# Moving one weight tile 16 bytes along its partition rows in a two-block transformer kernel

## The chip, the cores and the metric

The kernel runs on one core of one Trainium2 chip. The metric is the device time of one execution in microseconds (us). Single instructions are given in nanoseconds (ns). The profile comes from one execution that the hardware profiler recorded.

## The reference

Two transformer blocks are applied one after the other to one sequence of 512 tokens of width 1024, in float32. The first block projects the normalised input, runs a latent attention and a grouped attention with rotary angles, merges them with sigmoid gates, and then applies a squared-ReLU feed-forward of width 4096 and a gated embedding. The second block is a gated delta rule layer with a gated feed-forward of width 2816, followed by a forgetting-attention layer with another such feed-forward. Cut to the form in which the weights matter:

```python
z = rmsnorm(x, g_mix) @ w_in                 # ... attention, gates
x = x + merged @ w_o
u = relu(rmsnorm(x, g_mlp) @ w_up);  x = x + (u * u) @ w_down
...
gu = rmsnorm(x, g) @ w_ffn_in
x = x + rmsnorm((silu(gu[:, :2816]) * gu[:, 2816:]) @ w_ffn_out, g2)
```

Nearly all of the work is a product of a 512-row activation with a weight matrix.

## The kernel before

**Weights.** All weight matrices are packed on the host into 165 chunks, each at most 128 partitions by 2048 float32 values (8 KB of each partition). The chunks stream through a ring of two slots. For chunk n, SyncE loads it into `weights_raw` (line 199, up to two chunks ahead), ScalarE rounds it to the matmul's input type into `weights_high` (L223), and VectorE writes the remainder, raw minus high, into `weights_low` (L250). Chunk n uses slot n % 2 of each of the three tiles. SyncE waits for `low_ready` of chunk n - 2 before it loads chunk n, ScalarE waits until the last product that reads chunk n - 2 is done, VectorE waits for ScalarE, and TensorE waits for VectorE (`low_ready`). Three chunks are kept in tiles of their own, `early_high` and `early_low`.

**Products.** Each activation is also split into a high and a low part (`split`, `hidden`, `merged` and others). A product is then three matmuls that add up in one PSUM bank: high by high (L441), weight-high by activation-low (L442), and weight-low by activation-high (L443). At the start of some stages the same three stand at L452, L456 and L453. The first operand of `matmul` is the stationary one, loaded by a weight load (PEld), and the second is the moving one. In the names of the profile the moving operand stands first: `psum<-split,weights_low` has `weights_low` stationary. In the last feed-forward the two sides are exchanged, so `weights_low` is the moving operand there (L442, `psum<-weights_low,hidden`), and also in a few projections. Nearly every matmul of this kind has 128 stationary columns and 512 moving columns. One matrix has only 16 columns (the decay logits, `128*16`, where the piece of contraction tile k begins 64 * k bytes into the chunk) and one has 80 (`128*80`, the forget logits, whose piece begins at column 176 of 256, which is 704 bytes in).

**Order in memory.** Along each partition row the tiles stand in the order in which they are declared: `weights_raw`, `weights_high`, `weights_low` (16,384 bytes each), then `const` (259 values: an identity, a column of ones and others), `gains` (110 values), `conv` (96 values), a tile `arena_offset` that nothing reads or writes (40 values), `x_stream`, and the rest. Each tile begins at a multiple of 32 bytes, the same rounding that the class `Stage` reckons with:

```python
self.at += (4 * math.prod(shape[1:]) + 31) // 32 / 32
```

Rounded so, `const`, `gains`, `conv` and `arena_offset` take 1,056 + 448 + 384 + 160 = 2,048 bytes.

**Order of work.** Stages follow one another, each with its own program for every engine; the order within an engine is written out by hand. Nothing in it depends on addresses.

Of the kernel before, what the change touches and what calls it, by code (L numbers as in the profile page):

```python
# [4 lines left out]
P = 128  # L5
# [23 lines left out]
FOX_HEADS, FOX_HD = 16, 64  # L29
D_FF2 = 2816  # L30
CHUNK = 2048
SOLVE = 32
EXPONENT_LIMIT = 40.0
NEG = -1.0e30
# [19 lines left out]
for _name, _n in [("identity", P), ("heads_of_pair", 2), ("ones", 1), ("causal_bias", P),  # L54
                  ("earlier", P), ("before", P), ("not_after", P), ("eye", SOLVE * SOLVE)]:
    CONST_AT[_name] = (_col, _n)
# [5 lines left out]
def shape_constants():  # L62
# [3 lines left out]
    def put(name, value):  # L66
        at, n = CONST_AT[name]
        c[:, at:at + n] = value
# [11 lines left out]
    put("not_after", np.where(row <= col, EXPONENT_LIMIT, NEG))  # L80
    put("eye", np.eye(SOLVE).reshape(1, SOLVE * SOLVE))
    return c
# [20 lines left out]
class Chunk:  # L103


    def __init__(self, first, i=0, per_turn=0):
        assert per_turn % 2 == 0
        self.slot = first % 2
        self.number = first + i * per_turn if per_turn else first
        self.uses = first // 2 + 1 + i * (per_turn // 2) if per_turn else first // 2 + 1  # L110
        self.first, self.i, self.per_turn = first, i, per_turn
# [39 lines left out]
class Weights:  # L151


    def __init__(self, nc, enter, plan, packed):
        from concourse import mybir
        self.nc, self.plan, self.packed = nc, plan, packed
        f32, f32r = mybir.dt.float32, mybir.dt.float32r
        self.f32, self.sub = f32, mybir.AluOpType.subtract
        self.raw = enter(nc.sbuf_tensor("weights_raw", [P, 2, CHUNK], f32))
        self.high = enter(nc.sbuf_tensor("weights_high", [P, 2, CHUNK], f32r))  # L160
        self.low = enter(nc.sbuf_tensor("weights_low", [P, 2, CHUNK], f32r))
        self.loaded = [enter(nc.semaphore(f"weights_loaded_{s}")) for s in range(2)]
        self.high_ready = enter(nc.semaphore("weights_high_ready"))
        self.low_ready = enter(nc.semaphore("weights_low_ready"))

        self.products = enter(nc.semaphore("products_done"))
        self.apart = {}
        self.start = {}
        n = 0
        for name, segments in plan:  # L170
            self.start[name] = n
            n += sum(turns * len(items) for turns, items in segments)
        self.total = n
        self.width, self.tiles_before, tiles = [], [0], 0
        for _, segments in plan:
            for turns, items in segments:
                for i in range(turns):
                    for kt, cols, count in items:
                        self.width.append(kt * cols)
                        tiles += count  # L180
                        self.tiles_before.append(tiles)
# [177 lines left out]
def pack_weights(plan):  # L359

    chunks, shapes = [], []
    for name, segments in plan:
        shapes.append((name, [(turns, [(kt, cols, count) for kt, cols, _, count in items]) for turns, items in segments]))
        for turns, items in segments:
            for i in range(turns):
                for kt, cols, part, _ in items:
                    chunk = np.zeros((P, CHUNK), np.float32)
                    chunk[:, 0:kt * cols] = part(i).reshape(P, kt * cols)
# [23 lines left out]
def build_program(nc, w, plan, constants, tables, out):  # L392
# [4 lines left out]
    f32, f32r, bf16 = mybir.dt.float32, mybir.dt.float32r, mybir.dt.bfloat16  # L397
# [3 lines left out]
    enter = ctx.enter_context  # L401


    def place(name, at, shape, dtype=mybir.dt.float32):

        under = int(at * 256)
        if under == 0:
            with nc.sbuf_tensor(name, shape, dtype) as tensor:
                return tensor
        with nc.sbuf_tensor(name + "_under", [P, under], mybir.dt.float32), nc.sbuf_tensor(name, shape, dtype) as tensor:  # L410
            return tensor
# [5 lines left out]
    with ctx:  # L417
# [1 line left out]
        const = enter(nc.sbuf_tensor("const", [P, N_SMALL_CONST], f32))  # L419
        gains = enter(nc.sbuf_tensor("gains", [P, N_GAINS], f32))  # L420
        conv = enter(nc.sbuf_tensor("conv", [P, N_CONV], f32))
        enter(nc.sbuf_tensor("arena_offset", [P, 40], f32))
        x = enter(nc.sbuf_tensor("x_stream", [P, DT, T], f32))
        square_sum = enter(nc.sbuf_tensor("square_sum", [P, T], f32))
        psum = enter(nc.psum_tensor("psum", [P, 8, T], f32))
# [1679 lines left out]
        def gdn_project(ahead_of, split, qkv, z2, lower, columns, scratch, kept, spare, inverses):  # L2105
# [26 lines left out]
            with stage("gdn_in", 133) as s:  # L2132
# [35 lines left out]

                X, step_product, M = [scratch[:, 2 * n:2 * n + 2, :].rearrange("p a (b c) -> p (a b) c", c=SOLVE) for n in range(3)]

# [3 lines left out]
                with nc.Block() as block:  # L2174
                    @block.sync
                    def _(sp_):
# [20 lines left out]
                        for n in range(TT):  # L2197
                            sp_.wait_ge(lower_ready, 2 * n + 2)
                            for r in range(4):
                                at = slice(r * SOLVE, (r + 1) * SOLVE)  # L2200
                                sp_.dma_start(solver_rows[r, n].rearrange("h s t -> s h t"), lower[at, n, :, at]).then_inc(blocks_out, 16)
                            if n == 1:
                                weights.load(sp_, start + 13)
                        at = CONST_AT["eye"][0]
                        sp_.dma_start(X.rearrange("p a b -> p (a b)"), constants[:, at:at + SOLVE * SOLVE]).then_inc(eye_in, 16)
                        sp_.wait_ge(blocks_out, 16 * 4 * TT)
# [6 lines left out]
                        weights.load(sp_, weights.end("gdn_in"))  # L2213
                        sp_.wait_ge(taken, SOLVE - 1)
                        sp_.dma_start(inverse_out.rearrange("r n h i c -> (r n h) (i c)"), X.rearrange("p a b -> p (a b)")).then_inc(written, 16)
# [1110 lines left out]

        early = [place(name, at, [P, CHUNK], f32r) for name, at in (("early_high", 0), ("early_low", 8))]
        for name in ("ffn0", "fox_in", "ffn1"):
# [111 lines left out]
```

## Time and profile before

| | |
|---|---|
| time of the runs | 2163.68, 2167.99, 2168.05 us, median 2167.99 us |
| the profiled execution | 2162.32 us |
| its span, first to last instruction | 2160.5 us |
| mean granted TensorE clock | 0.987 of 2.4 GHz |
| DMA | 190.68 MB, mean share of the 16 engines 0.26 |

The span is what the trace shows, and 1.8 us of the execution lie around it. An engine's busy time is the union of its instructions' durations. Matmuls are pipelined: one is listed with 389 ns from its start to its end, while the next starts some 227 ns after it. For TensorE the distance between starts is therefore the number to read.

### The profile page before, as it was taken

How to read it: one execution, taken by the hardware profiler on the slowest of the kernel's cores; microseconds unless marked ns; L12 is line 12 of the kernel's file. 1: busy time of each engine (PE TensorE's matmuls, PEld its weight loads, DVE VectorE, ACT ScalarE, POOL GpSimd, SP SyncE). 2: the span in 40 equal slices, each digit the busy share in tenths (PEclk: the TensorE clock that was granted, in tenths of full speed). 3: DMA queues.
4: the chain of work that ended last, by engine and by line, in shares of the span. 5: the costliest groups of instructions: out<-in, count | busy, mean ns of one | idle time of the engine just before them, and what ended most of it. 6: DMA issues, size and time to landing. Idle time of an engine off the chain costs nothing. (4 is left out here: it accounts for less than half of the span.)

```text
span 2160.5 us, 26090 instructions
## 1 busy us (share of the span) xinstructions
PE 2095.5 (97%) x10710; PEld 1697.5 (79%) x10710; DVE 1146.3 (53%) x1706; ACT 816.6 (38%) x1169; POOL 38.4 (2%) x34
## 2 busy tenths in 40 slices
PE   8999999999999999999999999999999899999998
PEld 6876678888888887787878888887786577888886
DVE  5674765542542579888846444324634736444423
ACT  4324753331232465542534222213325734322212
POOL 0120000000000000000100000000000000000000
PEclk9999999999999999999999999999999999999999
DMA  4220012223223222233122222222240031222221
GB/s 177 86 83 35 2 59 99 94 95 109 85 96 103 91 81 100 108 117 97 40 98 74 95 95 94 95 96 95 98 173 23 1 118 59 98 98 98 98 98 68
DMA packets 43111, 190.68 MB, mean 88 GB/s; under 512 B 15520, under 2 KB 16224, under 8 KB 22384
## 3 DMA queue, kind: packets, MB, share of 16 engines
q1 hardware_dynamic: 40656, 184.78, 25.0%
q10 hardware_dynamic: 2336, 4.23, 0.6%
q8 instruction: 85, 1.39, 0.3%
q14 instruction: 34, 0.28, 0.0%
HBM read 185.25 MB, written 3.74 MB: 87 GB/s over the span
## 5 line engine op out<-in xcount | busy, mean ns | idle before, releaser
L250 DVE TENSOR_TENSOR weights_low<-weights_raw,weights_high 128x2048 fp32r<-128x2048 f32 (+1 forms) x161 | 365.8, 2272 | 565.4 <-ACT weights_high L223 565.3
L441 PE MATMUL psum<-split,weights_high 128*128 128x512 f32 x1448 | 568.3, 392 | 8.3 <-PEq L146 4.2
L442 PE MATMUL psum<-split,weights_high 128*128 128x512 f32 x1448 | 564.6, 390 | 0.0
L443 PE MATMUL psum<-split,weights_low 128*128 128x512 f32 x1448 | 564.6, 390 | 0.0
L223 ACT CAST weights_high<-weights_raw 128x2048 fp32r<-128x2048 f32 (+1 forms) x161 | 304.0, 1888 | 545.3 <-PE psum L443 504.7
L441 PEld LDWEIGHTS psum<-split,weights_high 128*128 128x128 f32 x1448 | 272.2, 188 | 70.3 <-issue 8.4
L443 PEld LDWEIGHTS psum<-split,weights_low 128*128 128x128 f32 x1448 | 272.0, 188 | 57.4
L442 PEld LDWEIGHTS psum<-split,weights_high 128*128 128x128 f32 x1448 | 272.0, 188 | 56.0
L443 PE MATMUL psum<-hidden_high,weights_low 128*128 128x512 f32 x256 | 99.6, 389 | 0.0
L441 PE MATMUL psum<-hidden_high,weights_high 128*128 128x512 f32 x256 | 99.6, 389 | 0.0
L442 PE MATMUL psum<-hidden_low,weights_high 128*128 128x512 f32 x256 | 99.6, 389 | 0.0
L2042 ACT ACTIVATE ring<-ring 128x512 f32<-128x512 f32 x44 | 27.8, 632 | 117.4 <-DVE ring L2072 117.4
L441 PE MATMUL psum<-hidden,weights_high 128*128 128x512 f32 x176 | 68.5, 389 | 0.0
L442 PE MATMUL psum<-hidden,weights_high 128*128 128x512 f32 x176 | 68.5, 389 | 0.0
L442 PE MATMUL psum<-weights_low,hidden 128*128 128x512 f32 x176 | 68.5, 389 | 0.0
L441 PE MATMUL psum<-weights_high,hidden 128*128 128x512 f32 x176 | 68.5, 389 | 0.0
L443 PE MATMUL psum<-hidden,weights_low 128*128 128x512 f32 x176 | 68.5, 389 | 0.0
L443 PE MATMUL psum<-weights_high,hidden 128*128 128x512 f32 x176 | 68.5, 389 | 0.0
L452 PE MATMUL psum<-split,weights_high 128*128 128x512 f32 x112 | 48.0, 428 | 17.3 <-DVE weights_low L250 10.2
L2530 DVE SCALAR_TENSOR_TENSOR gdn_spare<-psum,conv,gdn_spare 128x511 f32<-128x511 f32 (+2 forms) x72 | 53.8, 747 | 11.0 <-ACT gdn_spare L2363 9.3
L938 DVE TENSOR_REDUCE attn_small<-psum 128x1 f32<-128x512 f32 x64 | 42.5, 688 | 30.6 <-PE psum L876 30.6
L442 PEld LDWEIGHTS psum<-hidden_low,weights_high 128*128 128x128 f32 x256 | 48.0, 188 | 10.1
(485 smaller groups left out, 3081.4 us busy)
## 6 DMA issues: line engine op xcount, KB each, us to landing
weights_raw<-in_weights SPq DMA_DIRECT2D x161, 1024.0 KB, 4.9
minus_c<-minus_c_rows ACTq DMA_DIRECT2D x16, 256.0 KB, 7.3
x_stream<-in_x SPq DMA_DIRECT2D x4, 512.0 KB, 7.1
gdn_in_grown<-gdn_rows SPq DMA_DIRECT2D x4, 512.0 KB, 4.7
chain_grown<-gdn_rows SPq DMA_DIRECT2D x4, 512.0 KB, 3.7
out<-end_results SPq DMA_DIRECT2D x8, 256.0 KB, 2.1
table<-rope_tables SPq DMA_DIRECT2D x1, 1024.0 KB, 12.0
weights_raw<-in_weights SPq DMA_DIRECT2D x1, 768.0 KB, 4.2
```

What stands on the lines that cost most here:

```text
L223: self.nc.scalar.copy(self.high_of(chunk.first)[:, 0:width], self.raw[:, chunk.slot, 0:width]).then_inc(self.high_ready, 1)
L250: self.nc.vector.tensor_tensor(out=self.low_of(n)[:, 0:width], in0=self.raw[:, n % 2, 0:width], in1=self.high_of(n)[:, 0:width].bitcast(se ...
L441: nc.tensor.matmul(bank, wh, ah, start=first, stop=False)
L442: nc.tensor.matmul(bank, wh, al, start=False, stop=False)
L443: return nc.tensor.matmul(bank, wl, ah, start=False, stop=last)
L452: nc.tensor.matmul(psum[:, bank, :], wh[:, k, sl], xh, start=k == 0, stop=False)
L938: nc.vector.tensor_reduce(small[:, 0, u:u + 1], psum[:, u % 4, 0:n], AX.X, ALU.max, negate=True).then_inc(max_ready, 1)
L2042: nc.scalar.activation(self.tanh[:, f % 2, :], self.gate[:, f % 2, :], ACT.Tanh, scale=0.5).then_inc(self.tanh_ready, 1)
L2530: nc.vector.scalar_tensor_tensor(out=mixed[:, o % 2, back:T], in0=psum[:, bank_of(o), 0:T - back], scalar=conv[:, at:at + 1], in1=mixed[:, ...
```

## The change

`weights_low` becomes a tile that is 4 float32 values (16 bytes) longer, and its two slots begin 16 bytes behind its start. `arena_offset` shrinks from 40 to 32 values, so that `x_stream` and all that follows keep their addresses.

```diff
+LOW_OFFSET = 4
...
-        self.low = enter(nc.sbuf_tensor("weights_low", [P, 2, CHUNK], f32r))
+        low = enter(nc.sbuf_tensor("weights_low", [P, LOW_OFFSET + 2 * CHUNK], f32r))
+        self.low = low[:, LOW_OFFSET:].rearrange("p (s c) -> p s c", s=2)
...
-        enter(nc.sbuf_tensor("arena_offset", [P, 40], f32))
+        enter(nc.sbuf_tensor("arena_offset", [P, 32], f32))
```

The tile is now 16,400 bytes long, rounded up 16,416. So `const`, `gains` and `conv` begin 32 bytes further on than before, and 32 + 1,056 + 448 + 384 + 128 = 2,048 bytes bring `x_stream` to its old place.

## Rows read from the trace of the kernel before

**Rows 1.** The page, part 1: busy time, share of the span, instructions.

```profile
PE 2095.5 (97%) x10710; PEld 1697.5 (79%) x10710; DVE 1146.3 (53%) x1706; ACT 816.6 (38%) x1169; POOL 38.4 (2%) x34
```

**Rows 2.** The chain that ended last, from 1740 us to the end, by line.

```profile
by line: PE psum L443 30.0%; PE psum L441 29.9%; PE psum L442 29.9%; DVE end_results L1901 1.3%; PE psum L452 1.1%; PE psum L453 1.1%; PE psum L456 1.0%; PE psum L1832 0.8%; DVE end_results L1882 0.7%; DVE weights_low L250 0.5%; DVE last_en
```

**Rows 3.** Who reads or writes weights_low: ns min/median/max; first, last start.

```profile
L443 PEld LDWEIGHTS psum<-split,weights_low x1448: 147/188/330, 23.9 to 2031.0; 128*128 128x128 f32 x180, 128*80 128x80 f32 x1
...
L442 PE MATMUL psum<-weights_low,hidden x176: 389/389/390, 2031.7 to 2150.7; 128*128 128x512 f32 x176
L250 DVE TENSOR_TENSOR weights_low<-weights_raw,weights_high x161: 282/2291/2661, 7.9 to 2131.6; 128x2048 fp32r<-128x2048 f32 x158, 128x1536 fp32r<-128x1536 f32 x1, 128x1024 fp32r<-128x1024 f32 x1, 128x128 fp32r<-128x128 f32 x1
...
L442 PE MATMUL psum<-weights_low,split x128: 387/389/398, 955.0 to 1644.3; 128*128 128x512 f32 x128
```

**Rows 4.** Whole span: busy us (instructions) of those that touch weights_low; clock, DMA.

```profile
0.00:2160.50 2160.50, 996.69 (x2548) 480.22 (x2548) 365.84 (x161) 0.99 0.26 88
```

**Rows 5.** Timeline of PE, 1400.4 to 1402 us: weights stationary; start, duration.

```profile
1400.48 0.39 PE L441 MATMUL psum<-hidden,weights_high 128*128 128x512 f32 x1
1400.71 0.39 PE L442 MATMUL psum<-hidden,weights_high 128*128 128x512 f32 x1
1400.94 0.39 PE L443 MATMUL psum<-hidden,weights_low 128*128 128x512 f32 x1
...
1401.84 0.39 PE L441 MATMUL psum<-hidden,weights_high 128*128 128x512 f32 x1
```

**Rows 6.** Timeline of PE, 2050 to 2051.5 us: weights moving.

```profile
2050.07 0.39 PE L442 MATMUL psum<-weights_low,hidden 128*128 128x512 f32 x1
2050.30 0.39 PE L443 MATMUL psum<-weights_high,hidden 128*128 128x512 f32 x1
...
2051.43 0.39 PE L442 MATMUL psum<-weights_low,hidden 128*128 128x512 f32 x1
```

**Rows 7.** Timeline of PE, 1531.1 to 1534.5 us: 80 stationary columns.

```profile
1531.16 0.39 PE L441 MATMUL psum<-split,weights_high 128*80 128x512 f32 x1
...
1534.33 0.39 PE L443 MATMUL psum<-split,weights_low 128*80 128x512 f32 x1
```

**Rows 8.** Timeline of PE, 810.6 to 814.4 us: 16 stationary columns.

```profile
810.83 0.40 PE L441 MATMUL psum<-first_split,weights_high 128*16 128x512 f32 x1
...
814.31 0.27 PE L1661 MATMUL psum<-const,gdn_in_final_stat 128*128 128x128 f32 x1
```

**Rows 9.** Groups by line and form: VectorE with SBUF operands 12, 8, 4 bytes in.

```profile
L2530 DVE SCALAR_TENSOR_TENSOR gdn_spare<-psum,conv,gdn_spare 128x510 f32<-128x510 f32 x24 | 18.0, 748 | 0.8
L2530 DVE SCALAR_TENSOR_TENSOR gdn_spare<-psum,conv,gdn_spare 128x509 f32<-128x509 f32 x24 | 17.9, 748 | 0.8
L2530 DVE SCALAR_TENSOR_TENSOR gdn_spare<-psum,conv,gdn_spare 128x511 f32<-128x511 f32 x24 | 17.9, 746 | 9.3 <-ACT gdn_spare L2363 9.3
```

**Rows 10.** The instructions on gains: the same operation, 512 elements, aligned start.

```profile
L1793 DVE SCALAR_TENSOR_TENSOR ring<-psum,gains,factor x18: 739/744/747, 1132.3 to 1793.7; 128x512 f32<-128x512 f32 x18
```

**Rows 11.** Timelines of ACT and of DVE, 1386 to 1401 us.

```profile
1387.14 1.91 ACT L223 CAST weights_high<-weights_raw 128x2048 fp32r<-128x2048 f32 x1 [3.22 <-PE psum L443]
...
1398.02 1.91 ACT L223 CAST weights_high<-weights_raw 128x2048 fp32r<-128x2048 f32 x1 [7.46 <-PE psum L443]
...
1389.08 2.29 DVE L250 TENSOR_TENSOR weights_low<-weights_raw,weights_high 128x2048 fp32r<-128x2048 f32 x1 [4.44 <-ACT weights_high L223]
```

**Rows 12.** Who waited for whom, PE's: us in total, times, longest.

```profile
PE psum L452 <- DVE weights_low L250: 10.2, 1, 10.2
...
PE psum L441 <- DVE weights_low L250: 5.6, 7, 1.7
```

**Rows 13.** Whole span: busy us (instructions) of those that read const.

```profile
0.00:2160.50 2160.50, 114.17 (x888) 96.18 (x888) 1.30 (x6) 0.99 0.26 88
```

**Rows 14.** The instructions on const: columns of ones and of heads, whose starts differ.

```profile
L1135 PE MATMUL psum<-const,square_sum x48: 164/250/251, 22.8 to 1808.5; 128*128 128x1 f32 x48
...
L566 PE MATMUL psum<-const,row_squares x48: 165/251/252, 65.0 to 84.4; 128*128 128x2 f32 x48
```

**Rows 15.** Windows 62 to 157 and 1376 to 1496 us: busy of PE, PEld, DVE, ACT, POOL.

```profile
62.00:157.00 95.00, 93.69 (x501) 76.16 (x500) 66.03 (x89) 28.30 (x32) 20.26 (x16) 1.00 0.26 89
...
1376.00:1496.00 120.00, 119.84 (x529) 98.91 (x527) 34.07 (x22) 30.68 (x26) 0.00 (x0) 1.00 0.31 105
```

## The prediction

> **What bounds the kernel now.** I read the page first, then the chain, then everything that touches the moved tile. The page has TensorE busy for 97% of the span, VectorE for 53%, ScalarE for 38% [rows 1]. The chain from 1740 us on is 30.0 + 29.9 + 29.9 = 89.8% the three matmuls of a product, and 0.5% the subtraction that writes weights_low [rows 2]. So time is set by the distance between the starts of matmuls, and by the few places where TensorE waits.
>
> That distance is the number to watch. With weights stationary, six matmuls start between 1400.48 and 1401.84 us: 1.36 / 6 = 226.7 ns each [rows 5]. With weights moving, six take 2051.43 - 2050.07 = 1.36 us, again 226.7 ns [rows 6]. 512 columns at the granted 2.4 GHz (clock 1.00 in these stretches [rows 15]) are 213.3 ns, so each matmul has 13.4 ns on top of its columns. Weight loads take 188 ns [rows 3], which leaves 39 ns of each distance free.
>
> **The change part by part.** No instruction, semaphore, wait, DMA or byte of traffic is added or removed, and no queue changes its order. What changes is the start address of some operands. Four kinds of access touch moved tiles.
>
> 1. weights_low as stationary or moving operand: 2548 matmuls and as many weight loads [rows 4], of which 176 + 128 in two groups (and four more) have it moving [rows 3]. No row has a start 16 bytes off, so I bound the cost by rows with other starts. The piece with 80 stationary columns begins 704 bytes into its rows, an odd multiple of 64, while its moving partner begins in step with the tiles; its 14 matmuls take 1534.33 - 1531.16 = 3.17 us, 226.4 ns each [rows 7]: no difference. With 16 stationary columns, whose pieces start at multiples of 64 bytes, 15 matmuls take 814.31 - 810.83 = 3.48 us, 232.0 ns each [rows 8]: 5.3 ns more. The column count differs there too, and most of the 5.3 ns may be its, so I use them as an upper bound for what a start can cost. From below: at most all 13.4 ns could go, if they were two reads getting in each other's way. I take 0, because the distance is the same 226.7 ns for high and low, for stationary and moving, and for starts that are out of step by 64 bytes, which a conflict between two addresses would hardly give. The bounds are +5.3 and -13.4 ns, times 2548: +13.5 and -34.1 us.
>
> The Trainium skill speaks against zero here. Its page "TensorE: Matmul & The Clock Gate", section "Back-to-back issue gap", gives a gap of N/2.4 + 2.5 ns, 215.8 ns for 512 columns; the rows show 226.7, so this trace does not agree, and the 10.9 ns between them could be read as something that a better placement returns. By that page the sum would be an estimated -27.8 us in place of 0.
>
> 2. The subtraction that writes weights_low: 161 times, median 2291 ns [rows 3]. The nearest rows are VectorE operations whose SBUF operands start 4, 8 and 12 bytes in: 746, 748 and 748 ns for 511, 510 and 509 elements [rows 9], against 744 ns for 512 at an aligned start [rows 10]. So an odd start costs about 4 ns. 161 times 4 ns is 0.6 us of VectorE time. In a steady stretch it is covered: ScalarE begins its rounding at 1387.14, the subtraction ends at 1389.08 + 2.29 = 1391.37, and the chunk is read when the other slot's products end, at about 1398.02, where the next rounding begins [rows 11]. That is 6.6 us of cover, by TensorE working on the other slot. Without cover it counts at the 1 + 7 places where TensorE waits for it [rows 12]: 8 times 4 ns, 0.03 us. Behind the subtraction, SyncE's next load waits for low_ready; being 4 ns later it is lost in the same 6.6 us. Taken: 0.0 us, with 0 below.
>
> 3. const moves by 32 bytes, though the change's words say that all else stays. It is read by 888 matmuls [rows 13]. Two of its pieces already start in different places, the column of ones 520 bytes in and the two head columns 512 bytes in, and take 250 and 251 ns [rows 14]. Taken: 0; at 1 ns each either way it would be 0.9 us.
>
> 4. gains and conv are read as one value per partition, at starts that step by 4 bytes already; 18 such operations lie within 739 to 747 ns [rows 10]. Taken: 0.
>
> One more rule bears on item 2. The Trainium skill, "SBUF — State Buffer", section "Specifications (TRN2)", says that SBUF has 16-byte lines and that each crossing to a new line pays. A shift by 16 bytes is one whole line, so even the 4 ns of the odd starts would not arise; no row here has such a shift, so the trace neither confirms nor refutes it. By that page item 2 is an estimated 0 in place of 0.03 us.
>
> **The sum**: 2162.32 + 0 + 0.03 + 0 + 0 = 2162.4 us for an execution like the profiled one. That execution is 5.7 us below the median of the runs shown, 2167.99, and the four executions known lie between 2162.32 and 2168.05. I forecast for the median of new runs a value inside that band, nearer to the median than to the profiled one: 2167 us.
>
> **The rivals.**
>
> *A: matmuls that read the low half get slower.* If a stationary or moving read that is out of step with the tiles around it keeps TensorE at the distance seen in the 16-column piece, it costs the 13.5 us of item 1: 2162.3 + 13.5 = 2175.8 for an execution like the profiled one, 2181.5 from the median. For it speaks that the big tiles of before all stand in step modulo 2,048 bytes, so no row shows a pair out of step by less than 64 bytes. Against it speak the 80-column rows and that a weight load has 39 ns to spare. It decides from 1.7 ns per low matmul on, where 2548 of them make 4.3 us, 0.2%. Chance 0.07.
>
> *B: the subtraction gets slower.* It writes 2048 elements per lane while reading two tiles, and from now on the written place is out of step with the read ones. If each took twice 2291 ns, the 8 places where TensorE waits for it would grow by 2.29 us, 18.3 us together, and in stages where VectorE is busier, 66.03 of 95 us between 62 and 157 us [rows 15], more places would join. 2186 us or more from the median. Against it: starts at 4, 8 and 12 bytes cost 4 ns, not a doubling. It needs some 0.5 us per subtraction, 8 times 0.5 = 4.3 us, before it can be measured. Chance 0.03.
>
> *C: a conflict goes away.* If the 13.4 ns on top of the columns come from a weight load and a moving read meeting in memory, and 16 bytes part them, up to 34.1 us go, 2134 us from the median. The page on TensorE gives a nearly equal end, an estimated 2140 us. Against it speaks that the excess is still there with an 80-column and with a 16-column load, which read less than two thirds and an eighth of the bytes [rows 7, 8]; a conflict of reads should shrink with the bytes. Chance 0.04.
>
> *D: the change doesn't do what it says,* in that const, gains and conv move and not the low half alone. That is so by the sizes, but it is worth under 1 us either way and ends with my forecast.
>
> **How the numbers follow.** No measurable change holds 0.80. A measurement of this kernel can tell about 0.2%, 4.3 us, from no change; the executions of before alone differ by 5.7 us, so 0.06 is left for a difference of over 0.2% that has no cause in the change, half to each side. Faster: C 0.04 + 0.03 = 0.07. Slower: A 0.07 + B 0.03 + 0.03 = 0.13. The likeliest case's own range is 2161 to 2170 us. It holds 0.80 nearly alone; I widen it above to A, since the untried pairing is the largest unknown, and a little below for scatter: 2159 to 2182 us. C lies outside.
>
> **What the profile of the changed kernel would show.** If I am right: the distance of starts stays 226.7 ns where weights_low is stationary and where it is moving; weight loads of it stay at 188 ns; the subtraction stays within 4 ns of 2291 ns; the waits of TensorE for it stay at 10.2 and 5.6 us. Under A every third distance is longer, or all settle near 232 ns, and TensorE's busy time grows by 10 us or more with the same counts. Under B the subtraction's median grows visibly and the waits of TensorE for it with it. Under C the distances after or before the low matmuls fall towards 213 ns. What would make the prediction wrong is a dependence on the relative place of two tiles finer than 64 bytes, which no row of before can show.

## The result, and the profile after

The changed kernel is slower: 2191.64 us median of four runs (2182.59 to 2199.17) against 2166.6 us (2163.68 to 2168.05). The ratio is 1.0116, with a 95% interval of 1.0073 to 1.0158. Its own runs spread over 16.6 us, those of before over 4.4 us here and over 8.6 us (2159.76 to 2168.33) in all its undisturbed runs beside the experiments. The profiled execution took 2199.17 us, its span is 2197.4 us, 36.9 us more than before.

The first line is the page's busy times of the changed kernel. Its line numbers are two higher than before: L445, L443, L444 and L252 answer to L443, L441, L442 and L250.

```profile
PE 2134.7 (97%) x10710; PEld 1700.8 (77%) x10710; DVE 1147.3 (52%) x1706; ACT 816.7 (37%) x1169; POOL 38.4 (2%) x34
```

Against [rows 1] the counts are the same, VectorE and ScalarE are busy as long as before, and TensorE is busy 39.2 us longer. So the 36.9 us lie in TensorE's instructions and not in its waits.

The instructions on weights_low in the changed kernel (ns min/median/max, first and last start):

```profile
L445 PEld LDWEIGHTS psum<-split,weights_low x1448: 147/188/331, 24.6 to 2065.2; 128*128 128x128 f32 x180, 128*80 128x80 f32 x1
...
L444 PE MATMUL psum<-weights_low,hidden x176: 388/396/398, 2065.9 to 2187.7; 128*128 128x512 f32 x176
L252 DVE TENSOR_TENSOR weights_low<-weights_raw,weights_high x161: 284/2292/2530, 7.6 to 2168.1; 128x2048 fp32r<-128x2048 f32 x158, 128x1536 fp32r<-128x1536 f32 x1, 128x1024 fp32r<-128x1024 f32 x1, 128x128 fp32r<-128x128 f32 x1
```

A weight load still takes 188 ns and the subtraction 2292 ns in place of 2291 [rows 3]. The matmul with weights_low moving grew from 389 to 396 ns. TensorE's waits for the subtraction are as before, 10.0 and 5.1 us beside 10.2 and 5.6 [rows 12]:

```profile
PE psum L454 <- DVE weights_low L252: 10.0, 1, 10.0
...
PE psum L443 <- DVE weights_low L252: 5.1, 7, 1.1
```

What changed is the distance between starts. The timeline of PE in the changed kernel, in the stretch that answers to [rows 5]:

```profile
1450.06 0.39 PE L443 MATMUL psum<-hidden,weights_high 128*128 128x512 f32 x1
1450.29 0.40 PE L444 MATMUL psum<-hidden,weights_high 128*128 128x512 f32 x1
1450.53 0.39 PE L445 MATMUL psum<-hidden,weights_low 128*128 128x512 f32 x1
...
1452.15 0.40 PE L443 MATMUL psum<-hidden,weights_high 128*128 128x512 f32 x1
```

Nine starts take 2.09 us, 232.2 ns each, in place of 226.7 [rows 5]. And it is not every third distance that grew: between 1300 and 1500 us the mean distance behind L443, L444 and L445 is 230.8, 233.3 and 232.5 ns, so behind the matmuls that read only weights_high too. Over the whole trace the mean distance of 128 by 512 matmuls (those under 260 ns counted) is 231.5 ns against 226.9. For 3 times 2548 = 7644 matmuls, 4.6 ns each is an estimated 35 us, which is nearly all of the 36.9.

### The profile page after: what moved, and what is told of

Its sections match the earlier page's. It is cut to its first block and busy times, and to the rows that moved or that the text cites. A ratio compares the mean times of both kernels' runs of the same rounds, so it can differ in the third digit from the quotient of the medians.

```text
span 2197.4 us, 26090 instructions
## 1 busy us (share of the span) xinstructions
PE 2134.7 (97%) x10710; PEld 1700.8 (77%) x10710; DVE 1147.3 (52%) x1706; ACT 816.7 (37%) x1169; POOL 38.4 (2%) x34
## 5 line engine op out<-in xcount | busy, mean ns | idle before, releaser
L252 DVE TENSOR_TENSOR weights_low<-weights_raw,weights_high 128x2048 fp32r<-128x2048 f32 (+1 forms) x161 | 365.6, 2271 | 582.5 <-ACT weights_high L225 582.4
L443 PE MATMUL psum<-split,weights_high 128*128 128x512 f32 x1448 | 573.4, 396 | 8.6 <-PEq L147 4.5
L444 PE MATMUL psum<-split,weights_high 128*128 128x512 f32 x1448 | 572.2, 395 | 0.0
L445 PE MATMUL psum<-split,weights_low 128*128 128x512 f32 x1448 | 570.3, 394 | 0.0
L443 PEld LDWEIGHTS psum<-split,weights_high 128*128 128x128 f32 x1448 | 272.3, 188 | 77.6 <-issue 8.2
L445 PEld LDWEIGHTS psum<-split,weights_low 128*128 128x128 f32 x1448 | 272.3, 188 | 63.6
L444 PEld LDWEIGHTS psum<-split,weights_high 128*128 128x128 f32 x1448 | 271.9, 188 | 62.8
L444 PE MATMUL psum<-hidden_low,weights_high 128*128 128x512 f32 x256 | 101.1, 395 | 0.0
L445 PE MATMUL psum<-hidden_high,weights_low 128*128 128x512 f32 x256 | 100.8, 394 | 0.0
L443 PE MATMUL psum<-hidden_high,weights_high 128*128 128x512 f32 x256 | 100.6, 393 | 0.0
L445 PE MATMUL psum<-weights_high,hidden 128*128 128x512 f32 x176 | 69.6, 396 | 0.0
L444 PE MATMUL psum<-hidden,weights_high 128*128 128x512 f32 x176 | 69.5, 395 | 0.0
L444 PE MATMUL psum<-weights_low,hidden 128*128 128x512 f32 x176 | 69.3, 394 | 0.0
L445 PE MATMUL psum<-hidden,weights_low 128*128 128x512 f32 x176 | 69.3, 394 | 0.0
L443 PE MATMUL psum<-weights_high,hidden 128*128 128x512 f32 x176 | 69.2, 393 | 0.0
L443 PE MATMUL psum<-hidden,weights_high 128*128 128x512 f32 x176 | 69.2, 393 | 0.0
L454 PE MATMUL psum<-split,weights_high 128*128 128x512 f32 x112 | 47.5, 424 | 17.0 <-DVE weights_low L252 10.0
L443 PEld LDWEIGHTS psum<-hidden_high,weights_high 128*128 128x128 f32 x256 | 48.1, 188 | 11.5
```

The lines of the kernel that those rows point to most:

```text
L252: self.nc.vector.tensor_tensor(out=self.low_of(n)[:, 0:width], in0=self.raw[:, n % 2, 0:width], in1=self.high_of(n)[:, 0:width].bitcast(se ...
L443: nc.tensor.matmul(bank, wh, ah, start=first, stop=False)
L444: nc.tensor.matmul(bank, wh, al, start=False, stop=False)
L445: return nc.tensor.matmul(bank, wl, ah, start=False, stop=last)
L454: nc.tensor.matmul(psum[:, bank, :], wh[:, k, sl], xh, start=k == 0, stop=False)
```

## The experiments

Below, a tile is "at 16" when it begins 16 bytes further on than before, and two tiles are "in line" when both moved equally or, as the later runs show, by amounts that differ by 256 bytes. Two theories stood at first: (1) the relative place of the low half disturbs TensorE, (2) the shift of const, gains and conv does. Later ones were M (what counts is the place of a stationary operand against its moving one), S (that of the high half against the low half) and A (a tile's own address).

**const_only** moves const, gains and conv alone.

```diff
+        enter(nc.sbuf_tensor("before_const", [P, 8], f32))
         const = enter(nc.sbuf_tensor("const", [P, N_SMALL_CONST], f32))
...
-        enter(nc.sbuf_tensor("arena_offset", [P, 40], f32))
+        enter(nc.sbuf_tensor("arena_offset", [P, 32], f32))
```

> weights_low stays in its old place; an unused tile of 32 bytes ahead of const moves const, gains and conv by 32 bytes, and arena_offset gives the 32 bytes back. Theory 1 (the relative place of the low half is the cause): starts of matmuls 226.7 ns apart in every long stretch, time within 0.2% of before. Theory 2 (the shift of const, gains and conv is the cause): about 232.2 ns in the long stretches, 1 to 1.5% slower, as in the changed kernel.

Measured: 2163.93 us, ratio 0.9998 (0.9988 to 1.0009). Theory 2 is out. (The brackets here and below hold the 95% interval.)

**low_32, low_64, low_4** are the change with LOW_OFFSET = 8, 16 and 1, and arena_offset at 32, 24 and 32 values.

> As the change, but the low halves begin 32 bytes further on in place of 16. Theory 1a (what matters is the place modulo 32 bytes): 226.7 ns throughout, within 0.2% of before. Theory 1b (any step out of line with the neighbouring tiles by less than 64 bytes does it): about 232.2 ns in most stretches, about 1.2% slower. Theory 2 (const, gains, conv) gives 1.2% slower as well, so this run is to be read with the run that moves const alone.

> Only the low halves move, by 64 bytes. Theory M (weights and activations have to be in line modulo 64 bytes) and theory A (each tile's own address has to be a multiple of 64 bytes, as all were before): starts 226.7 ns apart, time within 0.2% of before. The 80-column piece of before, which begins 704 = 11 times 64 bytes in and ran at 226.4 ns, is why 64 and not more. A rival with a longer period (128 bytes up to 2,048): 1 to 2% slower.

> The low halves begin 4 bytes further on, a step inside a 16-byte line. M and A: out of line, so 1 to 2% slower; the extra line that each read then touches (one in 32 of a 512-byte load) could add 1 ns or less on top. If only whole lines of 16 bytes count (a step inside a line leaves the order of the lines nearly as it was), the time stays within 0.3% of before. The subtraction on VectorE: within 5 ns of 2291 ns by all theories.

Measured: low_32 2206.59 us, ratio 1.0198 (1.0179 to 1.0216). low_64 2192.56 us, 1.0132 (1.0116 to 1.0148). low_4 2205.58 us, 1.0193 (1.0178 to 1.0208). So 4 bytes cost as much as 32, and the expectation that 64 bytes are harmless failed for both theories that had it. The busy times of all engines in a 300 us window of low_64 (1200 to 1500 us) show it in a count: 1299 matmuls, where before had 1325 in an equal window of the same stage (1180 to 1480 us). Its columns are the window, its length, and busy us (instructions) of PE, PEld, DVE, ACT and POOL, then granted clock, DMA share and GB/s. First before, then low_64:

```profile
1180.00:1480.00 300.00, 300.00 (x1325) 248.43 (x1324) 115.65 (x105) 79.17 (x69) 0.00 (x0) 1.00 0.28 97
```

```profile
1200.00:1500.00 300.00, 300.00 (x1299) 243.72 (x1299) 110.87 (x101) 76.14 (x66) 0.00 (x0) 1.00 0.28 96
```

**high_16 and high_low_16** pad the high tile, the second the low tile too:

```diff
-        self.high = enter(nc.sbuf_tensor("weights_high", [P, 2, CHUNK], f32r))
+        high = enter(nc.sbuf_tensor("weights_high", [P, 4 + 2 * CHUNK], f32r))
+        self.high = high[:, 4:].rearrange("p (s c) -> p s c", s=2)
```

> Only the high halves begin 16 bytes further on; the low halves stay. Both theories S and M have this slower by 1 to 1.5%: S because the steps between high and low are again 16 bytes, M because two of three matmuls are out of line (M allows up to twice the cost of the change, some 2.4%). A third theory L (something peculiar to the low tile, as VectorE's write of it) expects no change.

> High and low halves both begin 16 bytes further on, so they are in line with each other and 16 bytes out of line with the activations. Theory S (the step from one stationary operand to the next, high to low, is what disturbs TensorE): 226.7 ns throughout, no change from before. Theory M (a stationary tile out of line with the moving tile is what disturbs it): all three matmuls are out of line, at least the 1.2% of the change, up to 3 times as much if the change paid for one third only.

Both expectations describe the kernels wrongly. The padded high tile is 32 bytes longer, so the low tile behind it moved as well: high_16 has the high halves at 16 and the low halves at 32 bytes, high_low_16 has them at 16 and 48. Measured: 2205.95 us, 1.0194 (1.017 to 1.0218), and 2205.3 us, 1.0192 (1.0175 to 1.0208). Neither tells S from M.

**arena_32 and weights_arena_32.** The first only raises arena_offset from 40 to 48 values, which moves all activations by 32 bytes. The second pads high and low by 8 values each and sets arena_offset to 32.

> All weight tiles, const, gains and conv stay; arena_offset grows by 32 bytes, so x_stream, square_sum and all activation tiles, and the three chunks kept apart, begin 32 bytes further on. Theories M and A both: about 233 ns between starts and 1.9% slower, as with the weights moved, except in the stretches that read the chunks kept apart, where M expects 226.7 ns (both sides moved together) and A expects 233 ns. A theory that the weight tiles alone matter: no change.

> High halves, low halves and all of the arena begin 32 bytes further on together; only the raw tile stays. Theory M (relative place of stationary and moving operand modulo 64 bytes): 226.7 ns, within 0.2% of before. Theory A (own address modulo 64 bytes): both operands are off, 233 ns or more, 1.9% slower or worse.

Measured: arena_32 2209.83 us, 1.0209 (1.0192 to 1.0226). With every weight tile untouched it is as slow as any, so it isn't something of the low tile or of how VectorE writes it. Where it reads the chunks kept apart, which moved together with the activations, it ran at 230.5 ns on the mean (139 distances), neither M's 226.7 nor A's 233. These matmuls alternate there, six by six, with six of a chunk that is out of line, so the stretch decides nothing. weights_arena_32 2208.74 us, 1.021 (1.0191 to 1.0228). It had the same fault as above: high at 32, low at 64, arena at 32. Among themselves these places are those of low_32, and the distances are alike too (228, 233 and 239 ns in turn in both), a first sign that only relative places count.

**both_16, both_64, all_32** lay high and low halves in one tile, so that they move together:

```diff
+        both = enter(nc.sbuf_tensor("weights_both", [P, 4 + 4 * CHUNK], f32r))
+        self.high = both[:, 4:4 + 2 * CHUNK].rearrange("p (s c) -> p s c", s=2)
+        self.low = both[:, 4 + 2 * CHUNK:].rearrange("p (s c) -> p s c", s=2)
```

(with 4, 16 and 8 values; arena_offset 32, 24 and 40).

> A correction first: in the two earlier kernels that padded the high tile, the pad also pushed the low tile on, so high_16 had the high halves at 16 and the low halves at 32 bytes, high_low_16 had them at 16 and 48, and weights_arena_32 had high at 32, low at 64 and the arena at 32. Here high and low halves lie in one tile that begins 16 bytes further on, so both are at 16 and the arena at 0. Theory M (weights against activations): about 233 ns, 1.9% slower. Theory S (high against low alone): 226.7 ns, no change.

> High and low halves both at 64 bytes, the arena at 0. low_64 was 1.3% slower. If that came from high and low being 64 bytes apart (S with a long period, M with a period of 64), this one is back at 226.7 ns and within 0.3% of before, as the 80-column piece (704 = 11 times 64 bytes in, high and low alike) ran in before. If M has a period above 64 bytes: 231 ns or more in the long stretches, 1.3% slower or worse.

> High and low halves, const, gains, conv and the arena all 32 bytes further on; only the raw tile stays. Theory M or S (relative places): 226.7 ns, within 0.2% of before. Theory A (own address modulo 64 bytes): 233 ns, 1.9% slower or worse. weights_arena_32 did not decide it, since its low halves were at 64.

Measured: all_32 2163.43 us, ratio 1.0 (0.9987 to 1.0012). With all operands 32 bytes on together nothing is lost, so theory A falls for steps of 32 bytes. The raw tile stayed, so its place against high and low doesn't matter either. both_64 2205.33 us, 1.0191 (1.0173 to 1.0209): high and low are in line with each other and 64 bytes out of line with the activations. S alone can't explain that; of the three theories M is left, with a period above 64 bytes. both_16 2197.07 us, 1.015 (1.0123 to 1.0176), between the two. Two windows of both_16, the feed-forward of the first block and that of the second, show that one kernel has both:

```profile
450.00:750.00 300.00, 300.00 (x1325) 248.43 (x1324) 115.24 (x109) 86.24 (x85) 0.00 (x0) 1.00 0.28 97
1200.00:1500.00 300.00, 300.00 (x1287) 242.93 (x1287) 110.06 (x99) 75.42 (x65) 0.00 (x0) 1.00 0.27 92
```

The first runs at 300 / 1325 = 226.4 ns, like before, and the second at 233.1 ns, with the same places.

**reads_alone** (one execution) has no engine but TensorE at work while the starts are read. It leaves out the whole computation and copies x to the output. Four prepared tiles are read in the order of the product, one line of the program for each set of offsets:

```python
for t in S: last = [(mm(banks[t], H(0, k, t % 2), A(0, k), start=k == 0, stop=False),
                     mm(banks[t], H(0, k, t % 2), B(0, k), start=False, stop=False),
                     mm(banks[t], L(16, k, t % 2), A(0, k), start=False, stop=k == 7)) for k in W][-1][-1]
```

> This kernel leaves out the whole computation; its output is a copy of x. TensorE alone reads prepared tiles in the order of the real product (high by high, high by low part, low by high), 72 matmuls for each of 35 sets of start offsets, then eight series with one matmul per step; no other engine works meanwhile. If the effect lies in TensorE's own two reads: about 226.7 ns with all offsets at 0, and 229 to 233 ns with the low halves at 4, 8, 16, 32, 48 or 64 bytes, in nearly the same size as in the full kernels. If it needs writes of VectorE, ScalarE or DMA beside it: 226.7 ns in every set. Time about 44 times 16.5 us and the first copy, some 750 us.

Measured: 679.49 us. The timelines of PE in reads_alone, the 12th and the last of each set of 72 starts: all at 0 (L74), low at 16 (L80), low at 64 (L86), low at 256 (L94), both at 64 (L104), and weights and activations all at 32 (L134).

```profile
27.05 0.39 PE L74 MATMUL psum<-moving_high,weights_low 128*128 128x512 f32 x1
...
40.65 0.39 PE L74 MATMUL psum<-moving_high,weights_low 128*128 128x512 f32 x1
...
77.82 0.39 PE L80 MATMUL psum<-moving_high,weights_low 128*128 128x512 f32 x1
...
91.76 0.40 PE L80 MATMUL psum<-moving_high,weights_low 128*128 128x512 f32 x1
...
129.01 0.40 PE L86 MATMUL psum<-moving_high,weights_low 128*128 128x512 f32 x1
...
142.88 0.40 PE L86 MATMUL psum<-moving_high,weights_low 128*128 128x512 f32 x1
...
196.98 0.39 PE L94 MATMUL psum<-moving_high,weights_low 128*128 128x512 f32 x1
...
210.58 0.39 PE L94 MATMUL psum<-moving_high,weights_low 128*128 128x512 f32 x1
...
280.81 0.39 PE L104 MATMUL psum<-moving_high,weights_low 128*128 128x512 f32 x1
...
294.81 0.40 PE L104 MATMUL psum<-moving_high,weights_low 128*128 128x512 f32 x1
...
534.86 0.39 PE L134 MATMUL psum<-moving_high,weights_low 128*128 128x512 f32 x1
...
548.46 0.39 PE L134 MATMUL psum<-moving_high,weights_low 128*128 128x512 f32 x1
```

Divided by 60 distances: 226.7, 232.3, 231.2, 226.7, 233.3 and 226.7 ns. No other engine works meanwhile; over 27 to 677 us of reads_alone, columns as in the windows above but without ACT:

```profile
27.00:677.00 650.00, 647.50 (x2774) 512.22 (x2773) 0.00 (x0) 0.00 (x0) 1.00 0.00 1
```

So the effect is TensorE's own, and it needs no write by VectorE, ScalarE or a DMA. It also has the size of the full kernel: 232.3 ns with the low halves at 16 bytes. And 256 bytes are in line again. Two more sets fit M well: with all activations at 64 the distance is 228.9 ns (L126), the same as with both weight halves at 192 (L108), and 192 is what 64 bytes to the other side are modulo 256.

Three series of reads_alone bear on the prediction's rows. With one matmul per step, all in line, 128 stationary columns ran at 226.7 ns, 64 columns at 230.0 and 16 columns at 231.7 ns. So with fewer stationary columns the distance was longer with nothing out of line.

**low_256** (LOW_OFFSET = 64, arena_offset 40, so the arena moves by 256 bytes too), **reads_pairs** (further series of the same kind, one execution; the computation is again left out) and **after_again** (the changed kernel once more) took up what was left.

> The low halves, const, gains, conv and the arena begin 256 bytes further on, raw and high stay. If only the places modulo 256 bytes count: 226.7 ns throughout, within 0.2% of before. If the tiles have to be in line over more than 256 bytes (512 to 2,048, as they all were before): 231 ns or more and 1 to 2% slower.

> Again the computation is left out and TensorE alone reads prepared tiles; the output is a copy of x. First 17 series of one matmul per step, the stationary operand 0 to 256 bytes from the moving one in steps of 16: 226.7 ns at 0, 16 and 256, 229 to 236 ns between. Then three series with 80 stationary columns: if the 80-column piece of before was in line by its own, 226.7 ns at 0 and at 192 bytes; if 192 bytes count as they do at 128 columns, 228.9 ns or more. Then the order of the stages' first chunk, with the low halves at 16 and 32 bytes. Last the product order with 8 different starts each for offsets 0, low 16, both 16: if a start decides whether a series settles, offset 0 settles at 226.7 ns in all 8, low 16 and both 16 in some and not in others; if not, all 8 of a kind end alike.

> The changed kernel once more, one look. If the start of a stretch decides whether it runs at 226.7 or at 232.2 ns, other stretches than in the first profile may run at 226.7 ns, and the time moves with their share, between 2180 and 2200 us: each 100 us of matmuls that settle save 2.4 us. If the place alone decided, the same stretches would run at 226.7 ns in both profiles.

Measured: low_256 2163.19 us, ratio 1.0004 (0.9991 to 1.0017). Its window from 1200 to 1500 us has 1326 matmuls, 226.2 ns:

```profile
1200.00:1500.00 300.00, 300.00 (x1326) 248.39 (x1325) 115.81 (x106) 82.26 (x75) 0.00 (x0) 1.00 0.30 100
```

In reads_pairs (725.76 us) one matmul per step ended at these mean distances, by how far the stationary operand stands from the moving one. Each column is one series of 48 matmuls per place:

| bytes | 0 | 16 to 64 | 80 | 96 | 112 | 128 | 144, 160 | 176 | 192 | 208, 224 | 240 | 256 |
|---|---|---|---|---|---|---|---|---|---|---|---|---|
| ns | 226.7 | 233.3 | 232.0 | 234.2 | 233.3 | 232.1 | 233.3 | 230.0 | 228.9 | 233.3 | 226.7 | 226.7 |

The expectation had 226.7 ns at 16 bytes, as the series of reads_alone with one matmul per step had run there; here it was 233.3 ns. So one series doesn't tell what a place always gives, and 240 bytes may be such a case as well. With 80 stationary columns it was 233.3 ns at 0 and 231.1 ns at 192 bytes. The order of a stage's first chunk ran at 226.7 ns in line, at 233.3 ns with the low half at 16 and at 231.8 ns at 32 bytes. With starts varied eight times, the product order at 0 settled at 226.7 ns in all eight; with the low half at 16 bytes it stayed at 232.2 ns in all eight; with both halves at 16 bytes two of eight settled at 226.7 ns and six at 233.3 ns. The timeline of PE in reads_pairs, the 12th and the last start of two of these six and two, the same offsets behind a short matmul of 64 (L171) and of 128 columns (L177):

```profile
589.36 0.39 PE L171 MATMUL psum<-moving_high,weights_low 128*128 128x512 f32 x1
...
603.36 0.39 PE L171 MATMUL psum<-moving_high,weights_low 128*128 128x512 f32 x1
...
623.76 0.39 PE L177 MATMUL psum<-moving_high,weights_low 128*128 128x512 f32 x1
...
637.36 0.39 PE L177 MATMUL psum<-moving_high,weights_low 128*128 128x512 f32 x1
```

14.00 against 13.60 us for the same 60 distances. The two differ only in the matmul ahead of them, and each keeps its distance to the end. It doesn't go by the length of that matmul alone: 128 and 192 columns led to 226.7 ns, 64, 96, 160, 224, 256 and 288 to 233.3 ns.

after_again took 2192.89 us, 6.3 us less than the first profiled execution. The same window of the two executions of the changed kernel, first the one of the result, then this one:

```profile
1200.00:1500.00 300.00, 300.00 (x1294) 242.47 (x1293) 113.32 (x104) 76.86 (x67) 0.00 (x0) 1.00 0.28 96
```

```profile
1200.00:1500.00 300.00, 300.00 (x1326) 248.47 (x1325) 115.62 (x105) 78.84 (x68) 0.00 (x0) 1.00 0.29 96
```

1294 matmuls are 231.8 ns each, 1326 are 226.2 ns. In the first execution the stretch from 1183.5 us on ran 1462 matmuls at 232.2 ns; in the second the same stretch ran at 226.7 ns, 1462 times 5.5 = 8.0 us less, and a few shorter stretches went either way. Other stretches came out alike in both, 232.2 ns between 420 and 760 us for one. So in some stretches of the changed kernel one execution settles and the next doesn't, with the same places. That the spread of its times is the sum of such cases is argued from these two traces.

None of the versions is faster than before, and no series of 128 by 512 matmuls with 128 stationary columns ran below 226.7 ns.

## Why the prediction was wrong

**The step that failed** is item 1, "I take 0". It costed the reads of weights_low at nothing because the distance was the same "for starts that are out of step by 64 bytes". The runs showed 4.6 ns on each of some 7644 matmuls in its place. The reason given rested on the piece with 80 stationary columns [rows 7], and there on 14 of its 24 matmuls. The same trace has the ones before them, from the second start to the tenth:

```profile
1529.30 0.39 PE L442 MATMUL psum<-split,weights_high 128*80 128x512 f32 x1
...
1531.16 0.39 PE L441 MATMUL psum<-split,weights_high 128*80 128x512 f32 x1
```

Eight distances take 1.86 us, 232.5 ns each. So the piece began at the distance of rival A and had settled by 1531.16 us, where the row begins. And in const_only, where weights and activations stand as before, it never settled. Its tenth to its last start:

```profile
1534.04 0.40 PE L442 MATMUL psum<-split,weights_high 128*80 128x512 f32 x1
...
1537.28 0.40 PE L444 MATMUL psum<-split,weights_low 128*80 128x512 f32 x1
```

That is 3.24 us for the 14 distances that took 3.17 us in rows 7, 231.4 ns each. all_32 and low_256, with the same relative places, have it near 231 ns too, and so has reads_pairs at 192 bytes (231.1 ns), which is what 704 bytes are modulo 256. With 128 columns 192 bytes cost 2.2 ns (228.9 ns in reads_pairs) and 64 bytes up to 6.6 ns. One row out of line that happened to have settled was no sign that places are free.

**Rival A had the mechanism**, and the end of the prediction its mark ("or all settle near 232 ns"). Its size was off by the number of matmuls: 5.3 ns was within 0.2 ns of the 232.2 - 226.7 = 5.5 of an unsettled stretch, but it was put on the 2548 matmuls that read the low half, 13.5 us, while the distance of all three matmuls grows, 7644 of them. That 5.3 ns came so near is luck: it was taken from the 16-column row, and 16 columns run at 231.7 ns with everything in line (reads_alone), so 5.0 of the 5.3 ns can come with the column count alone. Why the matmuls on high halves slow down too isn't shown; it may be that a disturbed matmul moves the start of the next, which then meets its own reads in another phase. In any case the price belongs to the whole series and not to the operand that moved. Put on all of them, A's own 5.3 ns would have been 40.5 us, 2162.3 + 40.5 = 2202.8 us for the profiled execution, where 2199.17 was measured. The last sentence of the prediction looked for a dependence finer than 64 bytes; 64 bytes themselves cost 1.3% (low_64).

**Item 2** (the subtraction) was right: 2292 against 2291 ns, with TensorE's waits for it nearly unchanged; at 4 bytes (low_4) it takes 2294 ns. **Item 3 and D** were right that const moves, and that this costs nothing (const_only, 0.9998). **Item 4** is contained in that run. **Rival B** is refuted by the same 2292 ns, where it needed some 500 ns more. Its sum has a slip: 8 times 0.5 us is 4.0 us, and 4.3 us need 0.54 us; nothing rests on it. **Rival C** didn't come: no place that was tried brought the distance below 226.7 ns. The 10.9 ns above the figure of the Trainium skill, "TensorE: Matmul & The Clock Gate", section "Back-to-back issue gap", were given back by none of these places; in reads_alone they stay when the same stationary and the same moving address are read over and over (226.7 ns). The clock of 1.00 that the prediction reads in [rows 15] for the stretch at 2050 us lies outside those two windows; the trace of before has 1.00 there too.

**The second rule cited**, that of the Trainium skill, "SBUF — State Buffer", section "Specifications (TRN2)", on 16-byte lines, agrees with the trace for the subtraction it was cited for, 2292 against 2291 ns. It doesn't foresee what happened to TensorE's reads, where a shift by one, two or four whole lines cost 1.2% to 2.1%. The Trainium skill, "TensorE: Matmul & The Clock Gate", section "Part 2: What happens when you issue a matmul", says that loading the next weights takes no read bandwidth from the running matmul. The runs don't fit that well: with only TensorE at work, the distance depends on how far apart the two operands stand.

**What stays open.** That it is a conflict of the weight load with the moving read in the memory is argued, not shown; no run reads only one of the two. What makes a series settle isn't known either. At 16 bytes three sets of reads_alone ran at 226.7 ns (high alone, both halves, one matmul per step) and most series of reads_pairs at 233.3 ns. In line, all series with 128 stationary columns ran at 226.7 ns but one: all tiles at 16 together (233.3 ns, where all at 32 and all at 64 ran at 226.7 ns). And the low half alone at 16 bytes settled in none of its ten series with TensorE alone, while long stretches of the changed kernel did settle with it. So something that the two small kernels leave out may bear on the settling.

## What to carry to other kernels

Where TensorE is the bound, place stationary and moving tiles in line modulo 256 bytes, and take a pad tile that nothing reads for what it may be: part of the timing. Read the distance between starts of matmuls, not their durations or busy share, and look whether it is the same in every stretch; two values in equal stretches, or a spread of runs about twice that of the sister kernel, were the mark here of series that settle or don't. Before a row is taken as proof that something costs nothing, read the whole piece it comes from: here the nine matmuls ahead of the row said the opposite. And when a pad goes in ahead of other tiles, work out the new address of each of them: three kernels of this study measured something else than was meant.

## What the runs showed that was not expected

- The distance between starts of 128 by 512 matmuls takes steady values, 226.7 ns in line (with one exception) and mostly 228.9 to 234.2 ns out of it, with a period of 256 bytes in the distance of the two operands. 4 bytes do it as well (low_4, 233.3 ns in reads_alone).
- 226.7 ns is 13.3 ns over the 213.3 ns of the columns at 2.4 GHz, and so is 120.0 ns over 106.7 for 256 moving columns in reads_alone: the same excess for both lengths, in line.
- A series settles within its first twelve matmuls in the two small kernels, some from the first distance on, or not at all; with both halves at 16 bytes the same reads ended at 226.7 or 233.3 ns behind different first matmuls.
- With fewer stationary columns the distance was longer with everything in line: 230.0 ns at 64 and 231.7 ns at 16 columns, against 226.7 ns at 128.
